# Transposing each head's sums out of PSUM behind the third probability tile, in a four-layer diffusion backbone on one core

## The reference

```python
def mla_expand(ckv, kpe, w_ukv, k_hn):
    kvu = (ckv @ w_ukv).reshape(B, T, N_HEADS, QK_NOPE + V_DIM)
    k_nope, v = kvu[..., :QK_NOPE], kvu[..., QK_NOPE:]
    k = rms_norm(concat([k_nope, broadcast(kpe)]), k_hn)   # over 128 + 64 values
    return k, v
# queries: q = rms_norm((cq @ w_uq).reshape(..., N_HEADS, 192), q_hn), then rotary on the last 64
s = einsum('bqhd,bkhd->bhqk', q, k) * 192 ** -0.5
p = softmax(s);  o = einsum('bhqk,bkhd->bqhd', p, v)
```

## Time and profile before

| | before |
|---|---|
| median of three executions | 1592.15 us (1591.52 to 1595.76) |
| the profiled execution | 1589.77 us |
| its span, first to last instruction | 1587.9 us |
| PE busy | 1538.3 us (97%) |
| DVE busy | 1113.5 us (70%) |
| ACT busy | 743.5 us (47%) |
| mean granted TensorE clock | 0.991 of full |
| the head loop, scores of head 0 to the last weighted sum | about 111 to 350 us |

### The profile page before, as it was taken

The page is one execution under the profiler, slowest core; times in us unless marked ns, Lnnn a source line. Parts: engine busy times, 40 slices in busy tenths (PEclk is TensorE's granted clock), DMA queues, the critical chain, the costliest instruction groups (busy, mean ns, idle before and its releaser), DMA issues.

```text
span 1587.9 us, 26535 instructions
## 1 busy us (share of the span) xinstructions
PE 1538.3 (97%) x10793; PEld 1484.9 (94%) x10793; DVE 1113.5 (70%) x1885; ACT 743.5 (47%) x1236; POOL 287.6 (18%) x344
## 2 busy tenths in 40 slices
PE   8999889899999999999999999999998999999998
PEld 6988678789999999999999899999998999999998
DVE  5656767684877854766468999998688558568553
ACT  4445445463544422443235766576375335335332
POOL 0011111000045633544253122231000000000000
PEclk9999999999999999999999999999999999999999
DMA  9322323122244543443343288985212312222222
GB/s 329 104 81 87 96 75 119 36 95 80 65 159 156 165 133 122 140 158 126 120 130 110 54 170 172 190 163 112 77 49 80 107 55 92 94 80 74 87 67 80
DMA packets 142465, 178.14 MB, mean 112 GB/s; under 512 B 13025, under 2 KB 121257, under 8 KB 141320
## 3 DMA queue, kind: packets, MB, share of 16 engines
q1 hardware_dynamic: 120128, 109.68, 21.8%
q0 software_dynamic: 21888, 66.66, 16.8%
q10 hardware_dynamic: 328, 0.10, 0.0%
HBM read 148.93 MB, written 2.79 MB: 96 GB/s over the span
## 4 chain that ended last, share of the span: by engine, by line
PE 79%; DVE 11%; DMA 4%; ACT 3%; issue 2%; SPq 1%; POOL 0%; DVEq 0%; POOLq 0%; ACTq 0%
PE PS L775 20%; PE PS L777 19%; PE PS L780 19%; PE PS L856 5%; PE PS L858 5%; PE PS L857 5%; DVE YACC L2846 4%; DMA ZACC<-ZTAP 3%; PE PS L1179 1%; PE PS L1136 1%; DMA MODS<-in_w_mod 1%; PE PS L1190 1%; DVE GP L2810 1%; PE PS L1155 0%; DVE TMP L2257 0%
## 5 line engine op out<-in xcount | busy, mean ns | idle before, releaser
L775 PE MATMUL PS<-HH,WH 128*128 128x320 f32 (+1 forms) x1168 | 269.5, 312 | 2.7 <-DVE HL L2268 2.2
L777 PE MATMUL PS<-HL,WH 128*128 128x320 f32 (+1 forms) x1168 | 266.1, 309 | 0.0
L780 PE MATMUL PS<-HH,WL 128*128 128x320 f32 (+1 forms) x1168 | 265.3, 308 | 0.0
L2394 DVE SCALAR_TENSOR_TENSOR X<-PS,MODV,X 128x128 f32<-128x128 f32 (+2 forms) x216 | 81.5, 434 | 183.9 <-PE PS L780 183.9
L775 PEld LDWEIGHTS PS<-HH,WH 128*128 128x128 f32 x1168 | 194.6, 188 | 7.0 <-issue 3.5
L777 PEld LDWEIGHTS PS<-HL,WH 128*128 128x128 f32 x1168 | 196.0, 188 | 0.0
L780 PEld LDWEIGHTS PS<-HH,WL 128*128 128x128 f32 x1168 | 195.8, 188 | 0.0
L2082 DVE TENSOR_TENSOR WL<-RAW,WH 128x2048 fp32r<-128x2048 f32 (+2 forms) x56 | 126.8, 2264 | 63.4 <-ACT WH L1494 63.2
L775 PE MATMUL PS<-HIDH,WH 128*128 128x320 f32 x704 | 162.4, 311 | 0.9 <-DVE HIDL L2326 0.9
L1850 ACT ACTIVATE BGW<-BGW,SC 128x512 f32<-128x512 f32 x112 | 80.7, 723 | 172.7 <-DVE BGACC L2216 122.4
L697 POOL TENSOR_TENSOR BGACC<-BGACC,BGW 128x512 f32<-128x512 f32 x97 | 132.8, 1369 | 157.4 <-ACT BGW L1850 156.2
(11 more groups left out here) (409 smaller groups left out, 3210.0 us busy)
## 6 DMA issues: line engine op xcount, KB each, us to landing
BGW<-in_w_mod POOLq DMA_DIRECT2D x112, 256.0 KB, 2.9
RAW<-in_ffn_w_gate SPq DMA_DIRECT2D x22, 1024.0 KB, 5.2
RAW<-in_ffn_w_up SPq DMA_DIRECT2D x22, 1024.0 KB, 5.2
MODA<-in_w_mod POOLq DMA_DIRECT2D x48, 256.0 KB, 3.8
RAW<-in_ffn_w_down SPq DMA_DIRECT2D x16, 768.0 KB, 4.6
RAW<-in_ffn_w_down SPq DMA_DIRECT2D x8, 1024.0 KB, 5.8
RAW<-in_conv_w_pw SPq DMA_DIRECT2D x16, 512.0 KB, 5.3
WL<-RAW POOLq DMA_DIRECT2D x8, 1024.0 KB, 9.8
```

Of the source, the lines that this page charges most:

```text
L775: mm(o, wh, xh, start=first, stop=False)
L777: mm(o, wh, xl, start=False, stop=False)
L780: ins = mm(o, wl, xh, start=False, stop=last)
L2394: ins = V.scalar_tensor_tensor(out=X[:, m, t:t + b - a], in0=tile2(n)[:, bank, a:b], scalar=g, in1=X[:, m, t:t + b - a], op0=ALU.mult, op1 ...
```

## The change

The first two steps of `head_norm` are split. A new function `head_turn` holds the wait for the sums and the transpose into HTURN, which also frees the PSUM slot; `head_norm` keeps the wait for the transpose and all that follows. `head_turn(h + 1)` is called behind the low part of the third probability tile (t = 2), ahead of `rotate_queries` and the low parts of tiles 3 and 4. For head 0 it is called directly ahead of `head_norm(0)`. No instruction is added or removed, and no tile changes place.

```diff
-            def head_norm(h):
+            def head_turn(h):
                 n = ("hsum", h)
                 filled(dve, n)
                 V.transpose(HTURN[:].rearrange("p t c -> p (t c)"), tile2(n)[:, 0, 0:(QT + NKT) * COLG]).then_inc(free_of(n), 1)
-                was_read(dve, n)
+
+            def head_norm(h):
+                was_read(dve, ("hsum", h))
                 both = slice(0, QT + NKT)
...
             values(0)
+            head_turn(0)
             head_norm(0)
...
                     if t == 2 and h + 2 == HEADS:
                         split_output(0)
                     if t == 2 and h + 1 < HEADS:
+                        head_turn(h + 1)
                         rotate_queries(h + 1)
```

## The result

The changed kernel takes 1578.12 us (median of four executions, 1574.72 to 1579.57) against 1591.84 for the kernel before: the ratio is 0.9908, with a 95% interval of 0.9883 to 0.9933. That is 13.7 us less, where 20 had been forecast. The profiled execution was the slowest of the four, 1579.57, with a mean granted clock of 0.992; the other three had 0.994 to 0.995.

What follows compares the result with a forecast made beforehand. PE, idle or slowed by the wait for the transpose HTURN, was taken as the bound. Even heads 15.2, odd heads 4.0 and head 7 0.7 sum to 19.9 us: median 1592.15 becomes 1572, forecast 1570 to 1577, range 1568 to 1580.

Steps and rivals of the forecast that it cites:

- rival A: Clock still falls in even heads' remaining idle; dear form, behind the spread, loses 2.4 us per head, 1579; chance 0.06.
- the prediction's own signs: Profile signs: no granted 0.50 in the head loop; wrong if QP or copies hold the scores a microsecond or more.
- What bounds the kernel: Head loop: PE waits for HTURN to free hsum's slot, 5.0 us in even heads, 1.34 in odd, 2.01 in head 7.
- The transpose at its new place: Even head on DVE: HTURN runs 159.3 to 159.85, ROPEQ starts 0.15 later, the chain to DIAGL ends 0.41 earlier.
- PE in the even head: ma0 starts at 160.74, DIAGL replaces HTURN as the wait, scores start at 170.98 instead of 175.66: gain 4.68 us.
- Then ma1, 1.00: Even head, behind the key spread: the second background product takes 1.00 us, so the scores start at 170.98.
- So each even head pays for the wait twice.: Kernel before, even heads: PE loses the 5.0 us idle and then runs at half clock, 168.0 to 170.5.
- Odd heads: Heads 1, 3, 5: the 1.34 us wait ahead of the first weighted matmul goes, 4.0 in all; bounds 0 and 4.0.
- Head 7: DVE's chain sets the end: DIAGL ends 0.21 earlier and the gain is 0.7 us; bounds 0 and 2.0.
- Queues passed: POOL's copies now precede QP's data: 0 to 0.5 us per even head, taken as 0; moved issues cost nothing.
- Given back later (B): Rival: a DMA-fed stage behind the loop keeps its old time, returning a third to half: 1579 to 1582; chance 0.08.
- slower (C): Rival: the clock stays at half through products following the scores; 17 us at half per even head gives 1598; chance 0.02.

Runs made afterwards that it cites:

- the run with the odd heads alone: Against the kernel before, the transpose stands early for heads 1, 3, 5, 7 alone: 1589.66 us, ratio 0.9984.
- the even-only run: Against the kernel before, the transpose stands early for heads 2, 4, 6 alone: 1581.44 us, ratio 0.9932.
- half of the copies: The changed kernel with POOL making four of eight background weight copies per head, the second product reusing the first four: 1573.49 us, ratio 0.9886 to the kernel before.

## Why the prediction came out as it did

The time, 1578.12, lies inside the range of 1568 to 1580 and just above the forecast's own 1570 to 1577. The mechanism of the gain was right; the gain came out a third below the sum. The time is in the range because the range reached past the forecast to take in rival A (1579). The profile shows A in all three even passes, and it had been given 0.06: so the hit owes something to luck, and more to a wide range than to the sum. By the prediction's own signs two things were wrong: there is granted 0.50 in the head loop, and in pass 1 copies hold the scores by over a microsecond (31.67 us against 29.61 with half of them).

- *What bounds the kernel.* Right. The slot of hsum held PE; all six waits are gone, and the run with the odd heads alone showed that the three small ones hung on the transpose too.
- *The transpose at its new place.* Right, and free: the 0.15 us by which I let it delay the rotary multiply did not appear (160.55 less 0.86 is 159.69, the old time).
- *PE in the even head.* Right up to the spread. "Half of its four matmuls follow that", 0.35, was mis-sized: behind DIAGL the last two take 0.61 to 0.73. The step that failed is "Then ma1, 1.00": at half clock it took 1.94, and the first scores were slow too, 1.6 us per head, 4.8 in all.
- *The rivals' prices.* A was given 0.06 and happened in full form behind the spread in each even head of the profile, though at 1.6 and not 2.4 us per head. The argument against it ("Idle waits of 1.34 and 2.01 in the other heads left matmuls at full pace") took a few waits that had gone well for a bound. Six profiled kernels have these waits: behind the 2.01 of pass 7 the clock fell in two of the six (19.33 and 19.37 us for 17.8), behind the 1.34 in none of 18. And the even-only run shows the same 1.4 + 0.4 with and without a fall.
- *"So each even head pays for the wait twice."* This reading of the kernel before was wrong in its effect. The half clock was there, but keeping the clock up gained 1.3 us (interval 0 to 3), because the copies ended at about the same moment. The change takes both away at once, as it issues the copies 5.9 us earlier in the pass, so the total of 4.68 was right (4.65 in the even-only run) although its parts hid one another.
- *Odd heads.* 4.0 forecast, 1.0 measured. 1.34 became 1.16 without copies in the way (the longer half of the spread accounts for it), 0.9 to 1.0 with them, and -0.9 in pass 1. The step that failed is "So 1.34 each": it left the copies out. I had checked the copies in the even heads alone, where they start 5.9 us earlier against a product 4.5 earlier. In an odd head the product moves up and its copies do not: from ma0's end to the product's end there were 7.8 us before, 6.5 were wanted after, 6.8 is what it took where no copy held it, and in pass 1 the copies made it 8.7.
- *Head 7.* 0.7 forecast, 0.73 measured.
- *Queues passed.* Right: QP never came last in the changed kernel. POOL's two issues of QP took 0.53 us each while DVE ran the norm, and its four copies 2.13 in all beside the second pair of low parts and the first rotary subtraction, against 2.12 before beside DIAGH and DIAGL. The two-input contention that the Trainium skill warns of ("SBUF — State Buffer", Who interferes with whom) did not show. I had read that section too narrowly: it also says that a `tensor_tensor` did not stall DMA issues when this was measured, and these numbers agree.
- *Given back later (B) and slower (C).* Neither happened.

## What to carry to other kernels

When a wait goes, ask of each thing that its reader's end releases (copies, transfers, other tiles) how long it takes, and whether it moves along with its user; if it doesn't, that is the next bound, in the heads where the wait was small above all. A half clock behind a wait is worth nothing by itself if something else ends at the same time, and a gain that leaves new idle time behind may lose part of it to the clock; put useful work into that time, by changing the order of the engine's own queue, before trusting the sum. In the new profile look at the passes of a loop one by one: here the three odd passes gained 1.0 us in sum, and one of them had got longer.

## What the runs showed of the hardware

- Idle stretches of 1.40 and 0.39 us on PE, with 0.6 us of matmuls between them, were followed by half clock in all three even passes of the changed kernel, in one of three with the even heads alone, and in one of three with half of the copies; with the longer one filled they were not followed by it in any of the nine passes of three runs. The fall cost 1.6 us (3.0 where it lasted longer). A single idle stretch of 2.01 us was followed by half clock in two of six profiles, at a cost of 1.5 us, and one of 1.34 us in none of 18 passes.
- Four copies of 256 KB, issued by POOL 0.53 us apart, let the product behind them end 7.0 to 9.2 us after the matmul that released them, wherever the product had to wait for them. What makes the difference is not shown.
- A float32 matmul of 128x128 by 128 columns runs as two instructions and takes about 0.225 us (21 in 4.85 us, 44 in 9.99), twice a transpose of the same shape (ten in 1.09 us).
